# A transformer step on one Trainium2 core: the first norm's scale and shift in transposed form, and rows of the last gate and norm kept on chip

## The reference, cut to what matters

```python
sh1, sc1, gt1, sh2, sc2, gt2 = split(silu(c) @ w_ada + b_ada, 6)   # one row for the prompt, 8 for the samples
h = rmsnorm(x, g_norm1) * (1 + sc1) + sh1
q, k, v, u, g = split(h @ w_in)                # w_in is 2048 x 5120
vn = layernorm(gelu(g)); att = three dilated attentions, combined
x = x + gt1 * (concat(att, gelu(u) * (spatial(vn) + b)) @ w_out)
h2 = rmsnorm(x, g_norm2) * (1 + sc2) + sh2
idx, gate = product-key top 16 of 16384 experts for each of 8 heads, from h2 @ w_query
x = x + gt2 * sum over (gate * gelu(expert_u[idx] . h2)) * expert_v[idx]    # 128 experts for each row
y = rmsnorm(x, g_final)
```

## Time and profile before

| | us |
|---|---|
| median of 3 runs (lowest, highest) | 3966.85 (3962.17, 3967.79) |
| the profiled execution | 3963.0 |
| its span, first to last instruction | 3961.3 |
| PE busy | 2893.1 (73%) |
| DVE busy | 2573.8 (65%) |
| POOL busy | 1622.9 (41%) |
| ACT busy | 610.8 (15%) |
| moved by DMA | 1510.60 MB, 381 GB/s over the span |

### The profile page before, as it was taken

How to read it: one execution, slowest core, us unless ns; L and a number is a source line. 1 busy time by engine, 2 the same in 40 slices (tenths; PEclk the granted TensorE clock), 3 DMA queues, 4 the chain that set the end, 5 groups by cost and what they waited for, 6 DMA issues and landing times.

```text
span 3961.3 us, 27382 instructions
## 1 busy us (share of the span) xinstructions
PE 2893.1 (73%) x8394; PEld 1225.7 (31%) x8394; DVE 2573.8 (65%) x3843; ACT 610.8 (15%) x1435; POOL 1622.9 (41%) x1188
## 2 busy tenths in 40 slices
PE   5799998869999965677678879855555555555555
PEld 1243445633334432233333345511111111111110
DVE  3110111986678878555555677899998988777675
ACT  1000110111111122233310011211111111000010
POOL 2000000325343455343344454456556656566563
PEclk8899999979999978888989989977777667777777
DMA  9978852889999999999999999999999999999997
GB/s 357 340 278 314 298 183 103 335 352 409 414 414 413 412 371 416 421 421 420 420 413 374 416 403 416 409 422 422 421 421 418 404 418 418 421 422 415 421 417 291
DMA packets 304851, 1510.60 MB, mean 381 GB/s; under 512 B 25591, under 2 KB 25591, under 8 KB 153831
## 3 DMA queue, kind: packets, MB, share of 16 engines
q0 software_dynamic: 160592, 1153.12, 70.7%
q1 hardware_dynamic: 140234, 332.53, 22.6%
q10 hardware_dynamic: 3880, 23.20, 1.5%
HBM read 1493.98 MB, written 13.94 MB: 381 GB/s over the span
## 4 chain that ended last, share of the span: by engine, by line
DMA 51%; PE 33%; issue 7%; DVE 6%; POOL 2%; ACT 1%; SPq 0%; POOLq 0%; DVEq 0%; ACTq 0%
DMA arena<-in_expert_v_dram,arena 43%; PE ps L844 10%; PE ps L503 7%; PE ps L663 6%; DMA arena<-in_w_ada_dram 3%; PE ps L612 3%; PE ps L594 3%; POOL arena L2015 2%; DMA arena<-in_expert_u_dram,arena 2%; DVE arena L1778 1%; DVE arena L1732 1%; DMA arena<-in_w_out_dram 1%; PE ps L491 1%; PE ps L656 1%; DMA arena<-in_w_query_dram 1%
## 5 line engine op out<-in xcount | busy, mean ns | idle before, releaser
L844 PE MATMUL ps<-arena 128*128 128x512 f32 (+1 forms) x2176 | 1378.4, 772 | 862.5 <-DMA arena<-in_expert_v_dram,arena 820.6
L1778 DVE CUSTOM_DVE_ANT_0 arena<-arena 128x2048 f32<-128x2048 f32 x544 | 1246.8, 2292 | 442.5 <-DMA arena<-in_expert_u_dram,arena 437.9
L2015 POOL DMA_INDIRECT arena<-in_expert_v_dram,arena x544 | 886.1, 1629 | 1051.6 <-PE ps L844 785.8
L844 PEld LDWEIGHTS ps<-arena 128*128 128x128 f32 (+1 forms) x2176 | 450.6, 225 | 1719.6 <-issue 1477.4
L2015 POOL DMA_INDIRECT arena<-in_expert_u_dram,arena x544 | 686.3, 1262 | 660.4 <-DVE arena L1778 373.5
L1732 DVE SCALAR_TENSOR_TENSOR arena<-arena 128x1024 f32<-128x1024 f32 x539 | 691.6, 1283 | 225.5 <-issue 198.2
L663 PE MATMUL ps<-arena 128*128 128x512 f32 x896 | 400.7, 600 | 0.0
L1223 ACT ACTIVATE arena<-arena 128x128 f32<-128x128 f32 (+1 forms) x544 | 205.0, 392 | 1087.2 <-PE ps L844 908.9
L503 PE MATMUL ps<-arena 128*128 128x512 f32 x640 | 281.7, 597 | 3.6 <-DMA arena<-in_w_in_dram 2.5
L612 PE MATMUL ps<-arena 128*128 128x256 f32 (+1 forms) x1024 | 245.7, 401 | 3.6 <-DMA arena<-in_w_query_dram 2.6
L663 PEld LDWEIGHTS ps<-arena 128*128 128x128 f32 x896 | 166.1, 190 | 237.2 <-issue 236.4
(11 more groups left out here) (217 smaller groups left out, 1485.1 us busy)
## 6 DMA issues: line engine op xcount, KB each, us to landing
arena<-in_w_ada_dram SPq DMA_DIRECT2D x96, 1024.0 KB, 14.5
arena<-in_w_in_dram SPq DMA_DIRECT2D x80, 1024.0 KB, 10.6
arena<-in_w_out_dram SPq DMA_DIRECT2D x32, 1024.0 KB, 5.1
arena<-in_w_query_dram SPq DMA_DIRECT2D x32, 1024.0 KB
arena<-in_cache_k_dram SPq DMA_DIRECT2D x24, 1024.0 KB, 11.6
arena<-in_cache_v_dram SPq DMA_DIRECT2D x24, 1024.0 KB, 13.5
arena<-in_expert_u_dram,arena POOLq DMA_INDIRECT x544
arena<-in_expert_v_dram,arena POOLq DMA_INDIRECT x544
```

Source lines behind the costliest of these rows:

```text
L844: ins = MM(ps[0:rows, c, :], diag[t % 4][:, 0:rows], v_slot[t % RING][:, c * NC:(c + 1) * NC], start=(j == 0), stop=last, skip_group_check ...
L1778: V.tensor_tensor_reduce(out=u_slot[s % RING], in0=u_slot[s % RING], in1=h2[b], scale=1.0, scalar=0.0, op0=ALU.mult, op1=ALU.add, accum_ou ...
L2015: nc.gpsimd.indirect_dma_start(out=slot[s % RING], out_offset=None, in_=table, in_offset=bass.IndirectOffsetOnAxis(ap=idx, axis=0),).then_ ...
```

## The change

Two things are changed.

1. Scale and shift of the first norm are no longer brought to the rows. The rows are only normalised (`normalize`, one multiplication by a scalar for each partition) and transposed early, after ada 0. The modulation rows of the eight tiles concerned are transposed too, on PE, and kept as `mod_t` (one column for each of 16 row groups, part and sequence). DVE then applies them to the transposed activations in place, four row groups at a time. The ada tiles are computed in pairs (scale piece, shift piece), so that after each pair one quarter of the activations is ready; the new list `QUARTERS` puts quarter q of in 0 and in 1 behind tiles 2q + 2 and 2q + 3 (behind tile 8 for the last), and the remaining 15 ada tiles in groups of 2 and 3 between in 2 and in 7. Tiles 0 to 7 are neither stored in DRAM nor read back. For the blocks of stage B the normalisation is due at steps 7 to 9 and the transposed form at 28.3 to 29.3; the SP queue has no scale or shift to load. The transposes of the spatial weights and sub-keys are moved behind ada 1.
2. For blocks 2, 3 and the samples the second gate's rows and the final gain are loaded once, into the three slots of the weight ring after the last query weights, and `finish` reads them there.

```diff
-TILES = [("ada", n) for n in range(11)]
-for _i in range(IN_T):
-    TILES.append(("in", _i))
-    for _ in range(0 if _i >= 8 else 2 if _i in (2, 4, 5, 6, 7) else 1):
-        if sum(k == "ada" for k, _n in TILES) < ADA_T:
-            TILES.append(("ada", sum(k == "ada" for k, _n in TILES)))
-while sum(k == "ada" for k, _n in TILES) < ADA_T:
-    TILES.append(("ada", sum(k == "ada" for k, _n in TILES)))
-TILES += [("out", n) for n in range(OUT_T)]
-TILE_AT = {key: i for i, key in enumerate(TILES)}
+ADA_SEQ = [4, 0, 5, 1, 6, 2, 7, 3] + list(range(8, ADA_T))
+QUARTERS = []
+def add_tiles(*tiles):
+    for kind, n in tiles:
+        QUARTERS.extend((kind, n, q) for q in range(4))
+add_tiles(("ada", 0), ("ada", 1))
+for _q in range(4):
+    add_tiles(*(("ada", n) for n in ((2 * _q + 2, 2 * _q + 3) if _q < 3 else (8,))))
+    QUARTERS += [("in", 0, _q), ("in", 1, _q)]
+for _i in range(2, 8):
+    add_tiles(("in", _i), *(("ada", n) for n in range(9 + (5 * (_i - 2)) // 2, 9 + (5 * (_i - 1)) // 2)))
+EARLY = len(QUARTERS)
+add_tiles(*(("in", i) for i in range(8, IN_T)), *(("out", n) for n in range(OUT_T)))
+QUARTER_AT = {key: i for i, key in enumerate(QUARTERS)}
...
-scale1_a, shift1_a = at(Z0, D), at(Z0 + D, D)
-scale1_b, shift1_b = at(MIX0, D), at(MIX0 + D, D)
...
+mod_t = const(2, KD, 1 + DECB)
...
+gate2_kept, gfin_kept, gate2_kept_s = at(W0, D), at(W0 + D, D), at(W0 + 2 * D, D, rows=NS)
@@ tensor engine @@
+    def mod_turn(n):
+        pe.wait_ge(mod_ready, n + 1)
+        turn_many(("mr", n), [(mod_row[n % 4][:, k * P:(k + 1) * P], 1 + DECB, P) for k in range(4)])
+    owed, turn_owed = None, None
...
+    for kind, n, q in QUARTERS[:EARLY]:
         if kind == "ada":
+            ada_quarter(n, q)
+        else:
+            if n < 2:
+                pe.wait_ge(quarter_ready, q + 1)
+            in_quarter(n, q)
+        if turn_owed is not None and (kind, q) != ("ada", 0):
+            mod_turn(turn_owed)
+            turn_owed = None
...
-                    wait_norm_turned(pe, [("hb", b, g) for b in range(2, BLOCKS) for g in range(4)])
+                    pe.wait_ge(hb_ready, 1)
@@ scalar engine @@
-        elif b == 1:
+        else:
             act.wait_ge(norm_h, 10)
-        if b:
             act.wait_ge(fin_y, b)
-        if b < NB_P:
-            act.dma_start(fin, mod_dram[0, 5 * D:6 * D].partition_broadcast(P)).then_inc(gate2_loaded, 16)
-        else:
-            row = mod_dram[1, 5 * D:6 * D]
-            act.dma_start(fin[0:NS, :], bass.AP(row.tensor, row.offset, [[6 * D, DECB], [0, DECT], [1, D]])).then_inc(gate2_loaded, 16)
+        act.dma_start(fin, mod_dram[0, 5 * D:6 * D].partition_broadcast(P)).then_inc(gate2_loaded, 16)
     def finish(b, s):
         r = ROWS[b]
         after = s - FINAL[b]
-        if after == -2:
+        if after == -2 and b < 2:
             load_gate2(b)
         if after == 3:
             act.wait_ge(u_done, FINAL[b] + 1)
...
             act.wait_ge(fin_x, b + 1)
             c = 66 + b
             A.activation(fin[0:r, :], h2[b][0:r, :], ACT.Square, accum_out=stat[0:r, c:c + 1]).then_inc(fin_sq, 1)
-            act.wait_ge(fin_sq, b + 1)
-            act.dma_start(fin, g_final.partition_broadcast(P)).then_inc(gfin_loaded, 16)
+            if b < 2:
+                act.wait_ge(fin_sq, b + 1)
+                act.dma_start(fin, g_final.partition_broadcast(P)).then_inc(gfin_loaded, 16)
@@ vector engine @@
+    def normalize(u, x):
+        r = NORM_ROWS[u]
+        s = stat[0:r, u:u + 1]
+        dv.wait_ge(norm_rt, u + 1)
+        link(V.reciprocal(s, s))
+        V.tensor_scalar(x[0:r, :], x[0:r, :], s, None, ALU.mult).then_inc(norm_h, 1)
...
+    def mod_turn(n):
+        part, g = ADA_SEQ[n] // 4, ADA_SEQ[n] % 4
+        bank = wait_turn_full(dv, ("mr", n))
+        src = ps[:, bank, 0:4 * (1 + DECB)].rearrange("p (k b) -> p k b", b=1 + DECB)
+        turn_taken(V.tensor_copy(mod_t[:, part, 4 * g:4 * g + 4, :], src), ("mr", n))
+        wait_turn_taken(dv, ("mr", n))
+        if part == 0:
+            for b in range(2):
+                wait_turn_taken(dv, ("h", b, g))
+            for k in range(4 * g, 4 * g + 4):
+                link(V.tensor_scalar(h_ta[:, k, :], h_ta[:, k, :], mod_t[:, 1, k, 0:1], mod_t[:, 0, k, 0:1], ALU.mult, ALU.add))
+            dv.sem_inc(quarter_ready, 1)
...
-    MIX_AFTER = max(n for kind, n in TILES[:TILE_AT[("in", 3)]] if kind == "ada")
-    owed = None
-    for kind, n in TILES[:TILE_AT[("in", U_A)]]:
-        if (kind, n) == ("in", 0):
+    for b in range(2):
+        dv.wait_ge(xa_loaded[b], 16)
+        mean_square(b, h_a[b])
+    for b in range(2):
+        normalize(b, h_a[b])
+    owed, turn_owed = None, None
+    for kind, n, q in QUARTERS[:EARLY]:
+        if turn_owed is not None and (kind, q) != ("ada", 0):
+            mod_turn(turn_owed)
+            turn_owed = None
+            for _ in todo:
+                break
+        if owed is not None:
+            ada_fold(owed)
+            turn_owed = owed if owed < 8 else None
+            owed = None
+        if kind == "ada" and q == 3:
+            owed = n
+        if (kind, n, q) == ("in", 1, 3):
             for _ in todo:
                 pass
-            dv.wait_ge(mod1_loaded, 32)
-            for b in range(2):
-                modulate(b, h_a[b], h_a[b], scale1_a, shift1_a)
-        if owed is not None:
-            ada_fold(owed)
-            for _ in todo:
-                break
-            if owed == MIX_AFTER:
-                mix_units_a()
-            if owed == 0:
-                for b in range(2):
-                    dv.wait_ge(xa_loaded[b], 16)
-                    mean_square(b, h_a[b])
-            owed = None
-        if kind == "ada":
-            owed = n
-        if (kind, n) == ("in", 1):
             dv.wait_ge(in_misc, 16 * (DECB + 3))
             dv.wait_ge(in_free, 4)
             for b in range(2):
                 ln_stats(b, v_a[:, b, :])
             for b in range(2):
                 ln_apply(b, v_a[:, b, :], ln_g_a, ln_b_a)
+        if (kind, n, q) == ("in", 3, 3):
+            mix_units_a()
...
-            yield T_NORM1 + (i if i < 2 else 3.5)
-            if i == 0:
-                dv.wait_ge(mod1p_loaded, 32)
-            if i == 2:
-                dv.wait_ge(mod1s_loaded, 32)
-            modulate(4 + i, x_b[i], x_b[i], scale1_b, shift1_b)
+            yield 7.0 + i
+            normalize(4 + i, x_b[i])
+        yield T_TURN1 + 2.3
+        for b in (2, 3):
+            for g in range(4):
+                wait_turn_taken(dv, ("hb", b, g))
+        for k in range(KD):
+            if k == 8:
+                yield T_TURN1 + 2.8
+            link(V.tensor_scalar(h_tb[:, k, 0:2 * P], h_tb[:, k, 0:2 * P], mod_t[:, 1, k, 0:1], mod_t[:, 0, k, 0:1], ALU.mult, ALU.add))
+        yield T_TURN1 + 3.3
+        for g in range(4):
+            wait_turn_taken(dv, ("hb", SB, g))
+        hs = h_tb[:, :, 2 * P:NB_COLS].rearrange("p k (b t) -> p k b t", t=DECT)
+        for part, op in ((1, ALU.mult), (0, ALU.add)):
+            link(V.tensor_tensor(hs, hs, mod_t[:, part, :, 1:1 + DECB].unsqueeze(3).broadcast_to([P, KD, DECB, DECT]), op))
+        dv.sem_inc(hb_ready, 1)
...
+            gate = fin if b < 2 else gate2_kept if b < NB_P else gate2_kept_s
...
+            gain = fin if b < 2 else gfin_kept
@@ sync engine @@
     load_in_b(0, 0)
     load_in_b(0, 1)
+    load_in_b(0, 2)
     sp.wait_ge(ww_used, 16)
-    sp.wait_ge(sca_full, PH)
-    load_mod(0, shift1_b, None, mod1p_loaded, None)
-    load_mod(1, scale1_b, None, mod1p_loaded, None)
-    load_in_b(0, 2)
-    sp.wait_ge(norm_h, 6)
-    load_mod(0, None, shift1_b, None, mod1s_loaded)
-    load_mod(1, None, scale1_b, None, mod1s_loaded)
-    sp.wait_ge(norm_h, 7)
...
+    sp.wait_ge(ww_used, W_QB + 16)
+    load_mod(5, gate2_kept, gate2_kept_s, kept_loaded, kept_loaded)
+    sp.dma_start(gfin_kept, g_final.partition_broadcast(P)).then_inc(kept_loaded, 16)
@@ gpsimd engine @@
     for n in range(ADA_T):
-        pool.wait_ge(mod_ready, n + 1)
-        pool.dma_start(mod_dram[:, n * NC:(n + 1) * NC], mod_row[n % 4]).then_inc(mod_stored[n % 4], 16)
-        if n == 7:
-            for i in range(4):
-                pool.wait_ge(mod_stored[i], 32)
-            for part, dst in ((0, shift1_a), (1, scale1_a)):
-                pool.dma_start(dst, mod_dram[0, part * D:(part + 1) * D].partition_broadcast(P)).then_inc(mod1_loaded, 16)
+        if n < 8:
+            wait_turn_full(pool, ("mr", n))
+        else:
+            tile = ADA_SEQ[n]
+            pool.wait_ge(mod_ready, n + 1)
+            pool.dma_start(mod_dram[:, tile * NC:(tile + 1) * NC], mod_row[n % 4]).then_inc(mod_stored[n % 4], 16)
         if n + 4 < ADA_T:
-            pool.wait_ge(mod_stored[n % 4], 16 * (n // 4 + 1))
+            if n >= 8:
+                pool.wait_ge(mod_stored[n % 4], 16 * (n // 4 - 1))
             load_bada(n + 4)
     for i in range(4):
-        pool.wait_ge(mod_stored[i], 16 * ADA_T // 4)
```

(1 more changed line is left out.)

122 lines of the change are left out of this document (61 added, 61 removed).

## The result

| | before | after |
|---|---|---|
| median (lowest, highest), us | 3966.48 (4 runs beside it) | 3927.03 (3925.83, 3931.54; 4 runs) |
| ratio to before, 95% interval | | 0.9909 [0.9898, 0.9921] |
| the profiled execution, its span | 3963.0, 3961.3 | 3931.54, 3929.8 |
| DVE busy, PE busy | 2573.8, 2893.1 | 2573.5, 2879.5 |
| moved by DMA | 1510.60 MB | 1502.58 MB |

The change makes the kernel 36 us faster by the ratio, 39 by the two medians. The forecast was 54 (3913): the right sign and inside the range, 14 us too good by the medians and 18 by the ratio. The profiled execution of after is the slowest of its four, 4.5 us over their median.

The account below looks back on a forecast made before the run. Stage B was taken as bound by bytes except in dips, stage A by PE or DMA with the other resting. 35 + 11 + 5 + 3 = 54 us gave 3909, 3913 in the median's terms, range 3893 to 3942.

Parts of the forecast that it names:

- stage A: Whole first stage under the new order: last ada fold at 414.4 us against 449.45, 35 us saved.
- norm of blocks 2 to 4: Stage B: DVE's idle 9.45 us and 13.9 of products go, 12.4 of replacement work comes, 11 us saved.
- kept rows: ends of blocks, very end: Second gate and final gain loaded once: 5 us of stream bytes, 3 us of waiting for the gain at the end.
- The first 44 quarters: Start of stage A: DMA paces rounds of 27.7 us and in 2 starts at 156 us instead of 220.2.
- I cost them at nothing: Stage A rounds: early transposes and turned modulation rows hide in PE's spare time; uncovered, the eight turns cost 8 to 16 us.
- In 2 to the last fold: Rest of stage A: 229.2 us becomes 258.4, with four more grouped tiles 21.0 and three late third tiles 5.4.
- Move as they are: Behind stage A: attention, out and the queries are the same work in the same order and simply move.
- DVE is the bound from 750 to 900 us: Stage B norm: DVE at 24.2 and 24.7 of 25 us, so the 11 us it saves counts.
- Rival 1: Stage B norm gives nothing back, lost to a full DVE, new waits or POOL: 3924, chance 0.15.
- Rivals 3 and 4: Stage A rounds at low clock: half the time, 3944, chance 0.07; at 1.2 GHz throughout, slower, 3974, chance 0.04.
- Rival 5: New order saves nothing in stage A, PE held by turned rows or a late quarter: 3948, chance 0.04.
- Rival 2: Better mixing: third tiles not late, norm recovers all 16 us of lost DMA; 69 us saved, 3898, chance 0.15.

Follow-up runs that it names:

- tables apart: The changed kernel with three of DVE's table pieces ahead of the first norm and the others behind odd ada tiles only: 3923.39 us, 0.9901 to the kernel before.
- The pair with quarters spread: The changed kernel with ada quarters spread, with and without DVE's table pieces moved out of the rounds: 3901.63 us (0.985) and 3908.46 us (0.986).
- quarters spread: The changed kernel with its last 60 ada quarters laid two or three behind each quarter of in 2 to in 7: 3908.46 us, 0.986 to before.
- stage A alone: The changed kernel with the norm of blocks 2 to 4 as before and without the kept rows: 3952.96 us, 0.9974 to before.
- row form: The changed kernel with the norm of blocks 2 to 4 as before, scale and shift stored and loaded again: 3948.29 us, 0.9962 to before.

## Why the prediction was right or wrong

The total was 14 to 18 us too good, and that is the sum of two larger errors with opposite signs: stage A 25 too good, the norm of stage B 10 too low. That the time fell inside the range is in part the luck of this.

| term | forecast | measured (ratios) |
|---|---|---|
| stage A | 35 | 10 |
| norm of blocks 2 to 4 | 11 | 21 |
| kept rows: ends of blocks, very end | 5 + 3 | 9.5 |

**The first 44 quarters** (in 2 at 156, measured 163). The step "I cost them at nothing" failed for the turned rows. I gave PE 4.7 us to spare in each round, and the sum behind it counted PE's busy time alone. It left out waits between small steps that sit in order on two engines: the copy of the bank by ACT (0.8), the sum and product on DVE, and the table piece ahead of them. The prediction priced the uncovered case, 8 to 16 us, and did not ask what DVE has queued at that moment. The run with the tables apart shows that this queue was the main cause: with it gone the rounds and the start of in 2 are where the forecast put them. The pair with quarters spread gives it 4.5 of the 7; the other 2.4 are matmuls at the lower clock behind the waits, which vary from run to run.

**In 2 to the last fold** (258.4, measured 268.3). The term "1.8 late, three times" was mis-sized: three groups lose 7, 9 and 7 us. The pitch of 2.77 us for a quarter held (420.28, 423.05, 425.77 in the last group), but I let the first refill land some 5 us after the group's start, and in the last group it came 11 after it. The trace shows two things ahead of it: the slot of the last in quarter is refilled first (issued at 409.04, landed 5.9 us later), and ACT's two stores of 512 KB (L930, issued from 410.16, landed 8.5 and 10.1 later) move beside it. The forecast had such a store near one group, with 2.8 us; the second and the third both have one. In the first group, without a store, the refill came at 6.3 us and the quarters behind it 3.1 apart. Some 4 us that I had carried over from before, the wait of 2.54 and the slow quarter behind it, did not recur. The run with quarters spread, which removes every one of these waits and shortens this stretch by 19 us, settles that they were the cause.

**"Move as they are"** failed too. Of 18.3 us at the last fold 15.5 reach step 0, and 10 the end of the run with stage A alone. The first part of this loss has a place: 3.6 us go directly behind the last fold, where PE comes out of the third group's waits at a granted clock of 0.50 (a little comes back before step 0). The other, some 5 us by the ratios, runs along the whole stream of gathers. It is not a law that early time is lost there: of the 22.5 us that spreading the quarters adds at step 0, 19 are there at the end by the ratios. A profiled execution's own scatter is of the size of this loss, and its cause stays open.

**The norm of stage B** (11, measured 21). The wait of 9.45 and the products, 3 x (0.16 + 2.35 + 2.29), together 23.9, went exactly (table: 39.1 - 15.3 = 23.8). What failed is the other side, 12.4 of replacement, of which in the end only 5.7 count: the three normalisations took 1.29 each and not 1.62, and were hidden altogether by the wait of 3.86 for ACT; the 8.8 us of products cost 8.9 up to step 31, and 3.3 of them were back by step 34. So 18 in the profile, and 2 more that the order before loses from step 20 to 34 (15.6 to 13.8 in the run with row form). The step "DVE is the bound from 750 to 900 us" was the error: it was read from stretches at both ends, and between them (800 to 825 us, DVE at 20.5 of 25) another engine's result sets a step.

**Kept rows** (8, measured 9.5): right within the interval, and by its parts as far as single profiles tell: against the run without them after has gained 5.7 us by step 543 (forecast 5) and 3.4 behind it (forecast 3).

**The rivals.** Rival 1 fell: the norm in stage B gives 21, not nothing. One way into it was the rule of the Trainium skill (SBUF — State Buffer, SBUF: two separate sides) that a one-input float32 operation on DVE takes the port pair that GpSimd needs to write descriptors. No loss by it shows here: the three new multiplications start at 731.3, 738.7 and 747.5 us, and the stretch around them moves as much as the same steps did before (after, then before):

```profile
730.00:750.00 20.00, 20.00 (x91) 17.04 (x91) 19.42 (x52) 4.27 (x9) 7.08 (x6) 1.00 0.86 334
745.00:765.00 20.00, 20.00 (x90) 16.63 (x88) 19.45 (x58) 4.27 (x9) 8.57 (x8) 1.00 0.81 321
```

They cost DVE's own time (4.1 us; three times 1.29 and a reciprocal of 0.15 are 4.3) and no more, and the 16 products lie in a stretch of 412 GB/s. Rivals 3 and 4 fell: the granted clock in the rounds was 0.81 and 0.95, and an in quarter took 7.1 to 9.0 us, never 13.9. The warning of the Trainium skill (TensorE: Matmul & The Clock Gate, HAM oscillation — how this bites in real kernels) that a loop whose matmuls wait for DMA falls back to half clock again and again holds here for single places, not as a steady state: 1 to 2 us for a quarter behind a wait, and 3.6 behind the last group. Rival 5 named the mechanism that cost stage A most, "held by the in-order waits on turned rows or a late quarter", and 10 of 35 is nearer to its nothing than to the forecast; its total (3948) did not come, and I gave it 0.04. Rival 2 was right on the norm, which gave 21 for its 16, but not because DMA recovered all: a hole of 332 GB/s is left, and the four loads of 2.6 MB and the wait of 3.86 make up for it (this split is worked out from the rows and was not tested apart).

## What to carry to other kernels

Work added to an engine that is full in one stretch is free if, further on, it waits for another engine; work on an engine with room is dear if it is queued behind something long at the moment its result is due. Read the waits up to the next point of meeting, not the share. When two streams share a ring of few slots, mix them slot by slot; whole tiles in turn made PE and DMA rest by turns, and mixing by quarters gave half as much again as the change itself had. And test the parts one by one even where the total is near the forecast, for it may be two errors that cancel.
